# Inverse levels of a chunked recurrence: the second tile of a pair half a level behind the first, and one filling group per level in place of two

## The reference

```python
def step(S, inp):                      # per head, S is 64 x 64
    r_t, w_t, k_t, v_t, a_t, b_t = inp
    sa = jnp.einsum('bhvk,bhk->bhv', S, a_t)
    S = S * w_t[:, :, None, :] + sa[..., None] * b_t[:, :, None, :] + v_t[..., None] * k_t[:, :, None, :]
    y = jnp.einsum('bhvk,bhk->bhv', S, r_t)
    return S, y
```

## Time and profile before

| | |
|---|---|
| median of 3 runs | 1547.15 us (1547.14 to 1547.16) |
| profiled execution | 1547.55 us, its span 1545.8 us |
| the recurrence stage | some 335 to 567 us of the span |
| inverse levels of one pair | 55.65 us, two pairs |

### The profile page before, as it was taken

One profiled execution on the slowest core, in us unless ns is written; L12 is line 12 of the kernel. 1 busy time (PEld: TensorE's weight loads), 2 busy tenths in 40 slices (PEclk: granted clock), 3 DMA queues, 4 the chain that ended last, 5 costly groups with the idle time before them and its releaser, 6 DMA issues.

```text
span 1545.8 us, 23866 instructions
## 1 busy us (share of the span) xinstructions
PE 1521.3 (98%) x9310; PEld 1098.0 (71%) x9310; DVE 1074.6 (70%) x2049; ACT 415.7 (27%) x791; POOL 131.6 (9%) x107
## 2 busy tenths in 40 slices
PE   9999999999999999999999999999999999999997
PEld 7885544457777777676545674587858888888886
DVE  5975857885556546687698993658678887785553
ACT  3345274531111113101465664103010000000001
POOL 0020020032002100000197000000000000000000
PEclk9999999999999999999999999999999999999999
DMA  7122111121111112322122221220222222223321
GB/s 281 68 81 82 55 51 54 49 67 57 43 57 57 57 47 98 123 96 82 61 76 82 68 83 66 85 82 28 74 80 91 84 82 82 85 97 92 91 86 69
DMA packets 48720, 121.62 MB, mean 79 GB/s; under 512 B 5408, under 2 KB 19488, under 8 KB 48352
## 3 DMA queue, kind: packets, MB, share of 16 engines
q1 hardware_dynamic: 47088, 115.89, 22.3%
q10 hardware_dynamic: 1296, 2.89, 0.5%
q0 software_dynamic: 224, 1.31, 0.2%
HBM read 117.98 MB, written 2.10 MB: 78 GB/s over the span
## 4 chain that ended last, share of the span: by engine, by line
PE 84%; DVE 13%; ACT 1%; issue 1%; DMA 0%; DVEq 0%; SPq 0%; ACTq 0%
PE bank L650 16%; PE bank L796 6%; PE opair L1455 4%; PE vpair L1455 4%; PE bank L1455 3%; PE apair L1455 3%; PE vpair L680 3%; PE opair L680 3%; PE opair L1484 2%; PE vpair L1484 2%; DVE arena L2076 2%; DVE arena L2085 2%; PE vpair L730 2%; PE apair L680 2%; DVE arena L2834 2%; PE apair L1484 2%
## 5 line engine op out<-in xcount | busy, mean ns | idle before, releaser
L650 PE MATMUL bank<-h,ring 128*128 128x512 f32 x560 | 254.1, 596 | 0.8 <-ACTq L1618 0.8
L650 PEld LDWEIGHTS bank<-h,ring 128*128 128x128 f32 x560 | 102.8, 190 | 115.7 <-issue 111.4
L2076 DVE TENSOR_TENSOR arena<-ring 128x512 f32<-128x512 f32 (+2 forms) x148 | 91.1, 615 | 73.3 <-DMA ring<-weights 48.1
L650 PE MATMUL bank<-arena,ring 128*128 128x512 f32 (+1 forms) x320 | 119.3, 515 | 2.0 <-ACT arena L1622 1.9
L2085 DVE SCALAR_TENSOR_TENSOR arena<-arena,cols 128x512 f32<-128x512 f32 (+1 forms) x129 | 94.9, 735 | 4.6
L650 PEld LDWEIGHTS bank<-arena,ring 128*128 128x128 f32 x320 | 57.9, 190 | 47.0 <-issue 40.3
L3117 POOL TENSOR_TENSOR arena<-arena 128x512 f32<-128x512 f32 x47 | 61.6, 1310 | 10.4 <-ACT arena L1930 6.9
L2076 DVE TENSOR_TENSOR arena<-arena 128x256 f32<-128x256 f32 (+1 forms) x114 | 57.6, 505 | 6.0 <-PE bank L1007 2.1
L3122 POOL TENSOR_TENSOR h<-h,sq 128x512 f32<-128x512 f32 x2 | 2.5, 1266 | 695.2 <-ACT sq L2040 695.1
L2020 ACT ACTIVATE arena<-arena 128x512 f32<-128x512 f32 x22 | 13.9, 630 | 127.7 <-DVE arena L2085 127.6
L2076 DVE TENSOR_TENSOR arena<-arena,ring 128x512 f32<-128x512 f32 (+2 forms) x74 | 45.0, 609 | 3.7 <-DVE arena L2076 0.6
(11 more groups left out here) (401 smaller groups left out, 3147.4 us busy)
## 6 DMA issues: line engine op xcount, KB each, us to landing
ring<-weights SPq DMA_DIRECT2D x169, 512.0 KB, 3.7
ring<-weights SPq DMA_DIRECT2D x36, 256.0 KB, 3.0
ring<-weights SPq DMA_DIRECT2D x68, 128.0 KB, 2.4
x<-xt SPq DMA_DIRECT2D x8, 512.0 KB, 8.4
ring<-weights SPq DMA_DIRECT2D x40, 64.0 KB, 2.0
cst<-cst_in ACTq DMA_DIRECT2D x1, 1056.0 KB, 7.6
arena<-memt SPq DMA_DIRECT2D x2, 512.0 KB, 6.3
arena<-mem2t POOLq DMA_DIRECT2D x1, 1024.0 KB, 5.0
```

The source lines that it names most:

```text
L650: last = mm(o[:, 0:n], weight(), src, start=c == 0, stop=c == len(srcs) - 1)
L2076: do(V.tensor_tensor(out, a, b, op), sig)
```

## The change

On TensorE the order of levels 1 to 5 is rewritten. Level 1: rb_gram, left products of both tiles, keys_by_values, fill 4, "a" and "o" of tile 0, fill 4. Then for l = 2 to 5 one run: left product of tile 0 of level l, "a" and "o" of tile 1 of level l - 1, left product of tile 1 of level l, "a" (not at l = 5) and "o" of tile 0 of level l; at l = 2 and 3 the transpose of bb or k; then fill 8. Behind level 5: "o" of tile 1, rk_gram, weighted(t0), fill 4. "a", "o" and, from level 2 on, the left products take their pair of banks for one tile at a time, with a read signal of their own. VectorE and ScalarE read in the same order: VectorE takes left 0, "o" 1, some gate groups, left 1, "o" 0, a weight sum, gate groups, a weight sum. ScalarE copies keys by values before the first XX, and then XX of tile 1 and of tile 0 per level. GpSimd's program and the DMA queues' are as they were. The amount of work is the same.

```diff
-        O_BEFORE = P_BEFORE + (2 * 5 + 2 * (2 + 2 + 2) + 2) * (NT // 2)
+        O_BEFORE = P_BEFORE + (2 * 2 * 5 + 2 * (2 + 2 + 2) + 2) * (NT // 2)
...
-                for l in range(1, 6):
-                    rows, next_rows, turned = CROSSED[l - 1], CROSSED[l], TURNED[l - 1]
...
+                def new_left(l, tiles):
+                    rows = CROSSED[l - 1]
                     o = take_pair("v")
-                    for i in range(2):
+                    for i in tiles:
                         pe.wait_ge(ml_ready.sem, 10 * p + 2 * (l - 1) + i + 1)
                         if l == 1:
                             pe.wait_ge(xx_ready.sem, 2 * p + i + 1)
                         else:
                             pe.wait_ge(xx_next.sem, 8 * p + 2 * (l - 2) + i + 1)
...
                     for ins in last:
                         v_done.inc(ins)
-                    fill(work, 4)
+                def new_right(kind, l, i):
+                    rows, turned = CROSSED[l - 1], TURNED[l - 1]
+                    yt = head(YT_[p][i], rows)
+                    old = head(XT_[p][i], TURNED[l - 2] if l > 1 else "b")
+                    o = take_pair(kind)
+                    pe.wait_ge(y_ready.sem, 10 * p + 2 * (l - 1) + i + 1)
+                    pe.wait_ge(xt_ready.sem, 12 * p + 2 * (l - 1) + i + 1)
+                    if kind == "a":
+                        for ins in quad_products(o, rows, old, yt, rows, None, slot_=i):
+                            a_done.inc(ins)
+                    else:
+                        for ins in quad_products(o, turned, yt, old, rows, CROSSED[l], slot_=i):
+                            o_done.inc(ins)
+
+                rb_gram(t0)
+                new_left(1, (0, 1))
+                keys_by_values(t0)
+                fill(work, 4)
+                new_right("a", 1, 0)
+                new_right("o", 1, 0)
+                fill(work, 4)
+                for l in range(2, 6):
+                    new_left(l, (0,))
+                    new_right("a", l - 1, 1)
+                    new_right("o", l - 1, 1)
+                    new_left(l, (1,))
                     if l < 5:
...
+                        new_right("a", l, 0)
+                    new_right("o", l, 0)
                     if l in (2, 3):
                         transposed(t0, bb if l == 2 else k)
+                    fill(work, 8)
+                new_right("o", 5, 1)
+                rk_gram(t0)
                 weighted(t0)
                 fill(work, 4)
...
+            def new_xx(p, i):
+                o = a_pair()
+                do(fn(XX_[p][i], heads_of(o[:, :, 4 * i * C:4 * (i + 1) * C]), ACT.Copy), xx_next)
+                a_read_inc(2)
+
...
-                for l in range(1, 6):
-                    if l == 2:
-                        weighted_values()
+                weighted_values()
+                new_xx(p, 0)
+                read_through(reading, GATED, u0 + 12)
+                for l in range(2, 6):
+                    new_xx(p, 1)
                     if l < 5:
...
+                        new_xx(p, 0)
...
+            def take_left(p, tiles):
+                o = v_pair()
+                for i in tiles:
+                    tt(YT_[p][i], chunk_product(o, i), mask_by_bank("ident64"), ADD, y_ready)
+                signal_now(v_read)
+                signal_now(v_read)
+
+            def take_right(p, i):
+                o = o_pair()
+                copy(XT_[p][i], chunk_product(o, i), xt_ready)
+                signal_now(o_read)
+                signal_now(o_read)
...
+                read_through(reading, GATED, u0 + 8)
+                take_left(p, (0, 1))
+                take_rb()
+                next_sums(1)
+                read_through(reading, GATED, u0 + 10)
+                take_right(p, 0)
+                next_sums(1)
+                for l in range(2, 6):
+                    take_left(p, (0,))
+                    take_right(p, 1)
                     read_through(reading, GATED, u0 + 4 + 4 * l)
...
+                    take_left(p, (1,))
+                    take_right(p, 0)
                     next_sums(1)
                     read_through(reading, GATED, u0 + 6 + 4 * l)
...
                     next_sums(1)
+                take_right(p, 1)
+                take_rk(t0)
                 read_through(reading, GATED, u0 + 28)
```

More of the change, by code:

```diff
@@ L1236, in _ @@
                 fill(work, 8)
-                for l in range(1, 6):
-                    rows, next_rows, turned = CROSSED[l - 1], CROSSED[l], TURNED[l - 1]
-                    xx_kind, xt_kind = (CROSSED[l - 2], TURNED[l - 2]) if l > 1 else ("b", "b")
-                    if l == 1:
-                        rb_gram(t0)
-                    if l == 2:
-                        keys_by_values(t0)
+                def new_left(l, tiles):
+                    rows = CROSSED[l - 1]
                     o = take_pair("v")
-                    for i in range(2):
+                    for i in tiles:
                         pe.wait_ge(ml_ready.sem, 10 * p + 2 * (l - 1) + i + 1)
@@ L1250, in _ @@
                             pe.wait_ge(xx_next.sem, 8 * p + 2 * (l - 2) + i + 1)
-                        last = quad_products(o, rows, head(ML_[i]), head(XX_[p][i], xx_kind), None, rows, slot_=i)
+                        xx = head(XX_[p][i], CROSSED[l - 2] if l > 1 else "b")
+                        last = quad_products(o, rows, head(ML_[i]), xx, None, rows, slot_=i)
                     for ins in last:
                         v_done.inc(ins)
-                    fill(work, 4)
-                    if l < 5:
[L1256 to L1271, removed]
@@ L2641, in _ @@
                 take_inverse_grams(p, 1)
-                for l in range(1, 6):
-                    read_through(reading, GATED, u0 + 4 + 4 * l)
[L2644 to L2650, removed]
+                read_through(reading, GATED, u0 + 8)
[8 more added lines that the diff above has]
+                    take_right(p, 1)
+                    read_through(reading, GATED, u0 + 4 + 4 * l)
+                    take_left(p, (1,))
+                    take_right(p, 0)
                     next_sums(1)
                     read_through(reading, GATED, u0 + 6 + 4 * l)
[L2653 to L2659, removed]
                     next_sums(1)
+                take_right(p, 1)
+                take_rk(t0)
                 read_through(reading, GATED, u0 + 28)
```

## The result

| | before | after |
|---|---|---|
| median of six runs (lowest to highest) | 1547.24 us (1547.14 to 1547.56) | 1552.3 us (1552.1 to 1552.76) |
| profiled execution; its span | 1547.55; 1545.8 | 1552.71; 1550.9 |
| first and second inverse stretch | 55.65, 55.65 | 57.76, 57.76 |
| TensorE busy in one stretch | 55.65 | 55.55 |

The change makes the kernel slower: the ratio is 1.0033, with the interval 1.0022 to 1.0043. The forecast was 1551.2, +0.26%.

A forecast was written before the change was run, and what follows sets the result against it. TensorE was taken as the bound, busy 1521.3 of 1545.8 us, without stalls to fill. Terms: -2.7 + 4.0 + 1.8 + 0.5 + 0.4 = +4.0, giving 1551.2 us (+0.26%); range 1546.8 to 1554.0, by its terms' bounds 1549.0 to 1553.5.

The forecast's parts named there:

- The saving: Merged runs and fills on TensorE: 0.34 us saved four times per pair, -2.7 us in all (bounds -2.0 and -3.3).
- Eight-yield fills: Sign in TensorE's timeline: merged fills of about 7.1 us; near 7.3 would make the gain wrong.
- the rival of the split groups: Each of 26 split groups costs its increments, at most 0.06 us: +1.6, 1552.8 us; chance 0.08.
- The first wait: Fourth block of each run waits for ScalarE's XX copy of tile 1: 0.5 us, eight runs, +4.0 (3.2 to 4.8).
- ScalarE decides, by little: At the fourth block, ScalarE's copy comes at 1.9 us from the run's start, VectorE's vpair read at about 1.8.
- The second wait: Levels 2 and 3: the transpose behind the run waits for ScalarE's copy, 0.45 us four times, +1.8 (1.2 to 2.2).
- The third: Level 5: "o" of tile 0 waits for VectorE to read opair, 0.25 us twice, +0.5 (0 to 0.8).
- two waits of "o" on VectorE: Sign expected in TensorE's list of waits: two of "o" on VectorE.
- The fourth: After the last eight-yield fill, VectorE reads the third gate quarter late, delaying a gate group: +0.4 us, both pairs (0 to 1.0).
- Only the first wait is real: Rival: transposes' bank and VectorE's readings come in time; +1.3, 1548.4 us, no measurable change; chance 0.24.
- The ways back fit into the run: Rival: XX copy and vpair read return within the two blocks before the fourth; -2.7, 1544.5 us; chance 0.07.
- Late engines: Rival: VectorE or ScalarE late at each pair's level 4 run, about 2.5 us each; +5, 1556 us; chance 0.08.

The follow-up runs named there:

- experiment 1: Changed kernel with the transposes of bb and k moved to the middle of the eight-yield fill: 1550.64 us, ratio 1.0023 to the kernel before.
- Experiment 4: Changed kernel with one yield of gate work between third and fourth block of each run, seven behind the run: 1549.96 us, ratio 1.0018 to the kernel before.
- experiment 3: Changed kernel where tile 1's left products of levels 2 to 5 read tile 0's XX (computes something else): 1550.79 us, ratio 1.0023.
- experiment 5: Experiment 4 plus transposes in the middle of the fill and VectorE reading the gate quarter ahead of the RK product: 1548.25 us, ratio 1.0008.
- experiment 2: Changed kernel with ScalarE copying tile 1's XX twice per level, the signal behind the second copy: 1556.49 us, ratio 1.0061 to the kernel before.
- experiment 6: Kernel before with both tiles in step, one run of XX, XT and next left products and one fill of eight per level: 1549.4 us, ratio 1.0014.
- experiment 8: Experiment 6 with one yield of gate work between the XT products and the next left products: 1548.9 us, ratio 1.0012 to the kernel before.
- 7: Experiment 6 with 64 or 128 padding instructions on TensorE's queue far ahead of the stage: 1548.34 us (ratio 1.0007) and 1548.85 us (1.0013).

## Why the prediction was right

**The saving** came, a little smaller. Eight-yield fills are 7.0 to 7.1 as said. A pair has 3 x 0.55 + 0.61 + 2 x 0.45 + 0.19 = 3.35 us of waits and is 2.11 longer, so it saves 1.24, both pairs 2.5 where I had 2.7 (0.31 and not 0.34 each time; 0.28 if the transposes are put at the 0.38 of experiment 1). Two readings do without this subtraction. Experiment 4 puts an edge at 0.28. And level 4, which has no transposes, takes 10.71 (387.50 to 398.21) where before it took 10.40 between these two rows, and its wait is 0.61, so 0.30 is saved:

```profile
387.44 0.69 PE L1119 MATMUL vpair<-arena 64*64 64x64 f32 x32
...
397.84 0.69 PE L1119 MATMUL vpair<-arena 64*64 64x64 f32 x32
```

A block costs 0.46 to 0.51 whether or not its group was split, so the rival of the split groups fell. For the rule of the Trainium skill, "TensorE: Matmul & The Clock Gate", section "The cost: per-tile semaphore tail", it means that this trace doesn't bear it out here.

**The first wait** was 0.55 per run and not 0.5 (0.61 at level 4, where ScalarE's copy starts 0.06 later), 4.5 us and not 4.0. The way back was 1.49 and not 1.40: of the difference 0.09 comes from the last step, ScalarE's end to TensorE's start, 0.14 here, where I had taken 0.05 from products of another shape. That ScalarE decides, by little, was right; experiment 3 has the distance at 0.24, where I had said 0.1 (1.9 against 1.8).

**The second wait** was 0.45 in the timeline, as forecast, and 1.5 for all four by experiment 1, against 1.8. In the list it stands on another line than that of the copy (L1717).

**The third** was 0.19 and not 0.25. Since it shows as no bracket, my statement that the list would have two waits of "o" on VectorE was wrong in form: they stand only in the starts.

**The fourth** was 0.13 at its gate group and 0.11 at the one behind it (1.92 against 1.81), 0.5 for both pairs against 0.4; experiment 5 shows its cause.

The sum by these terms is -2.5 + 4.5 + 1.8 + 0.4 + 0.5 = +4.7; the stage shows +4.82, with 0.14 more in the outputs of pair 2. That the sum closes is no proof, since the saving was got as what is left over; the proof is in experiments 1 to 5. The profiled runs differ by 5.16: the stage starts 0.19 earlier, and behind it 0.5 is added. That is a wait for weights that the kernel before has not, in a later stage:

```profile
PE bank L1007 <- DMA ring<-weights: 0.5, 1, 0.5
```

It is 0.6 in experiment 2, 0.4 in 4, 0.7 in 6, 1.1 with 64 padding instructions, 0.9 in experiment 8, and absent in experiments 1, 3 and 5 and with 128. I tried nothing on it, and what it depends on stays open. Of the 1.2 us by which the profiled execution lies above its forecast of 1551.5, this is 0.5 and the stage 0.8, of which the first wait is 0.5; the earlier start takes 0.2 off.

**The forecast's own range** doesn't follow from its terms. Their bounds add up to 1548.3 to 1554.0 and not 1549.0 to 1553.5, and of the range as given over a quarter, not the lowest fifth, lies within 0.2% of the time before. The result lies inside either.

**The rivals.** "Only the first wait is real" fell with experiment 1. "The ways back fit into the run" fell with the timeline and experiment 3: with ScalarE's copy out of the way VectorE's reading still makes the block 0.3 late, as the argument against it had said. "Late engines" fell with the list of waits: each XX wait is 0.44 at most.

**Why the idea didn't pay here.** Each merge saves 0.30, and it took with it the cover of a way back of 1.49. Putting cover in again (experiments 4 and 5) costs the edge again. Keeping both tiles in step (experiment 6) has part of the cover from the run itself, but ScalarE's two copies still hold back its left products, which leaves about 0.3 per pair, and its runs of 192 products stand still once in each pair. That no other order could keep the 0.30 isn't shown.

## What to carry to other kernels

Before two runs are merged, count for each product how many blocks lie between the last instruction of its operand's producer and itself, and hold that against the way back (here 1.49 us from the start of the producing block, some three blocks); the 0.30 saved per merge is lost as soon as a single way back shows by more. Read such a loss from the starts: the idle times in brackets showed 0.37 of 0.55, and nothing at all of 0.19. And when a wait is taken away, look for the next one behind it, which here kept 0.3 of 0.55.

## What the runs showed of the hardware that was not expected

In runs of 192 products of 64x64 in a row, with as many weight loads, TensorE stood still for 1.08, 1.21 and 0.85 us with nothing released (first pair of experiments 6 and 7). With one yield inside the run it was 0.42 in experiment 8 (128 products, yield, 64 products) and 0.34 in experiment 5 (96, yield, 64, in level 5). The change's own runs, which have 192 products too but half a microsecond of waiting among them, show none.

The kept traces have the place. Number TensorE's recorded instructions in order (products, weight loads and the semaphore instructions of its queue). The last product before the stop in the first pair is number 4289 in experiment 6, 4800 with 64 padding instructions and 5313 with 128. These are 193, 192 and 193 past a multiple of 256, and so, at 192 or 193, are all nine stops without a releaser in the stage in experiments 5 to 8. This explains the direction. With 64 instructions put in ahead, a given place of the stream falls on products 64 instructions earlier; TensorE doesn't stop at that place but at the next but one, some 512 further on (4800 - 4289 = 511), which is a level later. The traces also have a queue that carries instructions (the page of experiment 6, part 3: packets, MB, share):

```profile
q8 instruction: 74, 1.21, 0.3%
```

Its 74 packets are of 16384 bytes each, beside 19077 recorded instructions of TensorE, one packet to some 258 of them. Before each of the nine stops ends, a packet of this queue has ended, always 1.28 to 1.58 us earlier (in experiment 6 at 376.08, where TensorE goes on at 377.36).

The Trainium skill, "Runtime: NRT & Kernel Launch", section "Instruction fetch mechanics", says that the sequencer fetches instructions in blocks of 256 while it works, and that crossing from one block to the next is mostly hidden. The places and the packets agree with such blocks. Hidden it is in this stage of the kernels before and after, which show no such stop; it isn't in the long runs of experiment 6, where products follow every 15 ns (0.47 us for 32). So place, size and time all point to the fetch. What isn't shown is which crossings stop: experiment 6 passes another such place within a run, at 365.1, without one, and no run changed the fetch itself.
